# A two-layer attention and mixture-of-experts kernel: six experts with fixed blocks in place of four

## The chip, the cores and the metric

The kernel runs on one core of a Trainium2 chip. The metric is the device time of one execution in microseconds (us). The compute engines are PE (TensorE, with its weight loads shown as PEld), DVE (VectorE), ACT (ScalarE) and POOL (GpSimd). SP (SyncE) issues most of the DMAs, and POOL issues the indirect ones.

## What is computed

Two layers run over 384 tokens of width 1024 (three tiles of 128). Each layer is attention followed by a mixture of experts, and everything around the change lies in the second part:

```
scores = sigmoid(x @ w_router)                    # 384 x 64
pick the top 6 of 64 experts per token (by groups), weights normalised and scaled
for each expert e, over the tokens that picked it:
    gu = x[tok] @ w_gu[e]                         # 1024 x 512
    y  = (silu(gu[:, :256]) * gu[:, 256:]) @ w_down[e]   # 256 x 1024
routed[tok] += weight * y
out = layer_norm(alpha * x + gate * (routed + shared_expert(x)))
```

384 tokens with 6 experts each make 2304 rows over 64 experts, 36 per expert in the mean. An expert's weights are 2 MB (gate and up) and 1 MB (down) in float32, so every layer reads 192 MB of them.

## The kernel before, in words

**Blocks.** Rows are worked on in blocks of 128 rows. `plan_blocks` (line 40) makes the list. The first PRE = 4 blocks hold experts 0 to 3 alone, with 128 rows each. The other 60 experts are ranked by how many rows they got, and the ranks fill 28 blocks of three kinds: one expert with 128 rows, two with 64 each, or three with 64, 32 and 32. The order is (3, 1, 3, 2, 3, 1, 2), four times over. That makes NB = 32 blocks. The experts have a load number n from 0 to 63 in the order of the blocks; `LOADS` gives the rank that belongs to n, and `BLOCK_OF[n]` its block.

**Two ways to the rows of a block.** For the first PRE experts the slots come early: DVE writes a one-hot matrix per expert and tile (L1499), PE multiplies it with a column triple (L1039), DVE turns the outcome into indices (L1512, L1513), and POOL gathers (L1923, from the loop at L1934). All other experts go through memory: DVE works out the order of the experts and a place for each of a token's six choices (up to L1559), POOL scatters 18 sets of entries into `slots` (L1939), waits for them (L1942), loads the table back (L1944), DVE takes it apart (L1569, L1570, in `take_slots` at block 2), and only then can POOL gather block 4 and the later ones (L1951, after `slots_ready`). The gathered rows alternate between two buffers, `xg[0]` and `xg[1]`; blocks 2 and 3 use `gateb` in place of them.

**One block on PE** (loop at L1133): `gate_up(b)` (L1079: 8 steps over the width, each with one, two or four matmuls side by side, which run at once on parts of the array), `turn_rows(b+1)` (L1066, transposes of the next block's gathered rows), `down_rows(b-1)` (L1103), `turn_hidden(b)` (L1089). `gate_up(b)` waits for its weights; `turn_rows` waits for the gather. From block 8 to block 30 every second block also carries a step of the shared expert (L1116, L1121, L1128).

**Weights.** Gate-and-up weights go through a ring of NG = 4 buffers, down weights through ND = 6. SP issues in one fixed order. Before the routing it loads gate-and-up 0 to 3 and down 0 to 3 (L681 to L687). Then it waits for the order of the experts (`order_ready`) and for the entries (L702), loads down 4 and 5, and from there goes block by block: the down weights of block b (each after `down_rows` of the block that used its buffer, L707), then, after `gate_up(b)` (L711), the gate-and-up weights that go into the buffers which block b has just freed (L713). At block 5 it adds the shared expert's weights, at block 25 the vectors of the last normalisation. In layer 0 it goes on with two pieces of the next layer's input projection (L725).

**After the blocks** the results, scattered to memory by POOL (L1929), are read back (L741), summed by PE (L1186) and DVE, and normalised.

Of the kernel before, what the change touches and what calls it, by code (L numbers as in the profile page):

```python
# [16 lines left out]
TILES = 3  # L17
# [12 lines left out]
E = 64  # L30
# [3 lines left out]
FAR = 4096  # L34
NG = 4
ND = 6
PRE = 4


def plan_blocks():  # L40

    blocks = [[(n, P)] for n in range(PRE)]
    wide, half, third = iter(range(PRE, 12)), iter(range(12, 40)), iter(range(40, E))
    for _ in range(4):
        for kind in (3, 1, 3, 2, 3, 1, 2):
            if kind == 1:
                blocks.append([(next(wide), P)])  # L50
            elif kind == 2:
                blocks.append([(next(half), 64), (next(half), 64)])
            else:
                blocks.append([(next(half), 64), (next(third), 32), (next(third), 32)])
    assert all(next(left, None) is None for left in (wide, half, third))
    return blocks
# [5 lines left out]
BLOCK_OF = [n for n, b in enumerate(BLOCKS) for r in b]  # L62
# [130 lines left out]
def build(nc, a, o):  # L193
    soft = [(m, t, h) for t in range(TILES) for m in "BC" for h in (0, 3)]

    with ExitStack() as ctx:
# [58 lines left out]
        xg = [c(DM), c(DM)]  # L255
# [71 lines left out]
        gateb = c(2 * DM).rearrange("p (c d) -> p c d", c=2)  # L327
# [59 lines left out]
        def run_layer(l):  # L387
# [110 lines left out]
            def gather_of(b):  # L498


                if b < PRE:
                    return (xg + [gateb[:, 0, :], gateb[:, 1, :]])[b], first_gathered[b], 16
                return xg[b % 2], gathered[b % 2], 16 * ((b - PRE) // 2 + 1)

            def block_loads(b):
# [28 lines left out]
            def _(sp):  # L534
# [42 lines left out]
                for i in range(EARLY):  # L577
# [16 lines left out]
                    if i == 3:  # L594
                        at, n = CONSTS["empty"]
# [82 lines left out]
                                 ).then_inc(down_ready[n % ND], 16)  # L678

                sp.dma_start(wr, at_layer("w_router").rearrange("a (p k) e -> p (a k) e", p=P)).then_inc(wr_loaded, 16)  # L680
                for n in range(PRE):  # L681
                    if n == 2:
                        for i in range(next_n // 2, next_n):
                            load_mod(NEXT0 + i, MODC + i)
                    emptied(CHUNKS - NG + n)
                    load_gu(n, n)
                    load_down(n, n)  # L687

                sp.wait_ge(order_ready, 1)
                sp.wait_ge(xm_saved, 16 * TILES)  # L690
                sp.wait_ge(xmT_ready, 4 * TILES)
                expert = {}

                def loaded(n):
                    if n not in expert:
                        r = LOADS[n]
                        expert[n] = sp.value_load(by_rank[0:1, r:r + 1], min_val=0, max_val=E - 1)
                    return expert[n]

                for b in range(NB):  # L700
                    if b == 0:
                        sp.wait_ge(entries_ready, 1)  # L702
                        for n in range(PRE, ND):
                            load_down(n, loaded(n))
                    for n in block_loads(b):
                        if n >= ND:
                            sp.wait_ge(y_full, BLOCK_OF[n - ND] + 1)  # L707
                            load_down(n, loaded(n))
                    gu_now = [n for n in range(NG, E) if BLOCK_OF[n - NG] == b]
                    if gu_now:  # L710
                        sp.wait_ge(gu_full, b + 1)  # L711
                    for n in gu_now:
                        load_gu(n, loaded(n))  # L713
                    if b == SHARED_LOAD:
                        sp.wait_ge(residual_ready, TILES)
                        sp.dma_start(shared_gu, at_layer("w_shared_gu").rearrange("a (p k) n -> p (a k) n", p=P)).then_inc(shared_loaded, 16)
                        sp.dma_start(shared_down, at_layer("w_shared_down").rearrange("a (k p) n -> p (a k) n", p=P)).then_inc(shared_loaded, 16)
                    if b == NORM_LOAD:
                        sp.wait_ge(sgu_full, TILES)
                        load_norm(1, G2)  # L720
# [1179 lines left out]
            def _(pool):  # L1900
# [19 lines left out]
                def gather(b):  # L1920

                    rows_in, landed, count = gather_of(b)
                    pool.indirect_dma_start(rows_in, None, scratch_x, bass.IndirectOffsetOnAxis(ap=slot_idx[:, 0, b:b + 1], axis=0),  # L1923
                                            bounds_check=TOK - 1, oob_is_err=False).then_inc(landed, 16)
# [6 lines left out]

                pool.wait_ge(xm_saved, 16 * TILES)
                pool.wait_ge(first_ready, 1)
                for b in range(PRE):  # L1934
                    gather(b)
                pool.wait_ge(table_empty, 16)
                pool.wait_ge(entries_ready, 1)
                for j in range(TILES * TOPK):
                    pool.indirect_dma_start(slots, bass.IndirectOffsetOnAxis(ap=place_i[:, j:j + 1], axis=0),  # L1939
                                            entry[:, j, :], None, bounds_check=P * NCOL - 1, oob_is_err=False  # L1940
                                            ).then_inc(entries_sent, 16)
                pool.wait_ge(entries_sent, 16 * TILES * TOPK)  # L1942
                by_row = slots.rearrange("(p c) v -> p c v", c=NCOL)
                pool.dma_start(table, by_row[:, 0:NB, :]).then_inc(table_loaded, 16)  # L1944
# [77 lines left out]
```

## Time and profile before

| what | value |
|---|---|
| median of 3 runs | 1990.85 us (1979.93 to 1992.41) |
| the profiled execution's own time | 1993.09 us |
| its span, first to last instruction | 1991.4 us |
| mean granted TensorE clock | 0.862 of full speed |
| PE / DVE / ACT / POOL busy | 78% / 28% / 16% / 10% of the span |
| DMA | 576.84 MB, 290 GB/s in the mean |

The profile cuts the span in 40 slices of 49.8 us. In two runs of slices (the tenth to the nineteenth and the thirtieth to the thirty-eighth) DMA is at 90% or more and moves 320 to 425 GB/s: these are the blocks of experts of the two layers. Matmuls are pipelined, so a busy PE is not PE at its peak.

### The profile page before, as it was taken

The page shows a single profiled execution, that of the slowest core. Times are in us where ns is not written, and L with a number is a line of the kernel's source. Part 1 is how long each engine was busy: PE and PEld are TensorE (multiplying, and loading weights), DVE is VectorE, ACT ScalarE, POOL GpSimd, SP SyncE. Part 2 cuts the span into 40 slices and gives each one's busy share as a digit, 9 for nine tenths or more (in the row PEclk, how much of TensorE's full clock was granted, in tenths as well). Part 3 has the DMA queues.
Part 4 walks back from the last instruction along what each step waited for, and adds up shares of the span by engine and source line. Part 5 has one row for each costly group of instructions (what it writes and reads, how often), then busy time and mean ns, then how long its engine had stood idle before and what let it go on. Part 6 is the DMA issues. An engine that isn't in the chain of part 4 may idle for free. (4 is left out here: it accounts for less than half of the span.)

```text
span 1991.4 us, 20055 instructions
## 1 busy us (share of the span) xinstructions
PE 1555.8 (78%) x7633; PEld 796.9 (40%) x7633; DVE 555.6 (28%) x1120; ACT 319.9 (16%) x626; POOL 200.8 (10%) x196
## 2 busy tenths in 40 slices
PE   4797998798587886986669889878758768788684
PEld 1586564453132332332238756545313323233231
DVE  0534332551011111111373444166101101111125
ACT  0322341210000000000122324311000000000000
POOL 0000000051011011100101000004201101101100
PEclk8897699788799898988789979987879988889797
DMA  7624345558999999999845443363599999999965
GB/s 291 190 105 179 131 143 217 226 194 320 417 417 417 395 407 412 408 379 410 325 152 153 143 172 101 126 249 138 210 425 405 414 416 406 398 395 397 418 265 221
DMA packets 114687, 576.84 MB, mean 290 GB/s; under 512 B 41662, under 2 KB 44238, under 8 KB 73500
## 3 DMA queue, kind: packets, MB, share of 16 engines
q1 hardware_dynamic: 94012, 534.36, 67.5%
q0 software_dynamic: 20512, 41.09, 5.5%
q8 instruction: 63, 1.03, 0.2%
q14 instruction: 36, 0.29, 0.0%
q10 hardware_dynamic: 64, 0.07, 0.0%
HBM read 565.10 MB, written 40.39 MB: 304 GB/s over the span
## 5 line engine op out<-in xcount | busy, mean ns | idle before, releaser
L1079 PE MATMUL bank<-ring,arena_a 128*32 128x512 f32 (+2 forms) x2432 | 520.7, 698 | 224.8 <-DMA ring<-in_w_expert_gu 221.7
L1079 PEld LDWEIGHTS bank<-ring,arena_a 128*32 128x32 f32 (+2 forms) x2432 | 174.9, 146 | 537.4 <-issue 537.4
L1608 DVE SCALAR_TENSOR_TENSOR arena_a<-arena_a,slot_w,bank 128x256 f32<-128x256 f32 x64 | 30.8, 481 | 649.2 <-ACT arena_a L1859 646.3
L1103 PE MATMUL bank<-arena_b,arena_a 128*32 128x512 f32 (+2 forms) x800 | 205.8, 599 | 3.0 <-DVE arena_a L1617 3.0
L1859 ACT ACTIVATE arena_a<-bank 128x256 f32<-128x256 f32 x64 | 24.7, 386 | 907.6 <-PE bank L1079 907.6
L1929 POOL DMA_INDIRECT scratch_y<-arena_a,slot_idx x64 | 65.9, 1030 | 920.2 <-DVE arena_a L1625 919.0
L858 PE MATMUL bank<-win_hi,xmT_hi 128*128 128x512 f32 (+1 forms) x288 | 109.0, 379 | 16.3 <-DVE arena_a L1228 11.2
L1103 PE MATMUL bank<-arena_a 128*32 128x512 f32 (+2 forms) x416 | 116.0, 595 | 0.0
L1624 DVE COPY arena_a<-bank 128x512 f32<-128x512 f32 x64 | 44.3, 692 | 248.8 <-PE bank L1103 248.8
L859 PE MATMUL bank<-win_hi,xmT_lo 128*128 128x512 f32 (+1 forms) x288 | 109.6, 381 | 0.0
L860 PE MATMUL bank<-w_lo,xmT_hi 128*128 128x512 f32 (+1 forms) x288 | 109.1, 379 | 0.0
L998 PE MATMUL bank<-ring,xmT 128*128 128x512 f32 x192 | 86.1, 611 | 6.4 <-ACTq L1818 6.4
L1103 PEld LDWEIGHTS bank<-arena_b,arena_a 128*32 128x32 f32 (+2 forms) x800 | 61.7, 130 | 67.8 <-issue 64.3
L1066 PE MATMUL bank<-cst,arena_a 128*128 128x128 f32 x480 | 68.0, 287 | 17.9 <-DMA arena_a<-scratch_x,slot_idx 17.9
L1066 PEld LDWEIGHTS bank<-cst,arena_a 128*128 128x128 f32 x480 | 55.7, 146 | 60.8 <-issue 43.3
L801 PE MATMUL bank<-ring,condT 128*2 128x512 f32 x384 | 63.7, 782 | 14.3 <-DMA ring<-in_w_mod 14.3
L1923 POOL DMA_INDIRECT arena_a<-scratch_x,slot_idx x60 | 64.0, 1067 | 74.5 <-DVE slot_w L1513 54.3
L1219 DVE TENSOR_TENSOR w_lo<-ring,win_hi 128x2048 fp32r<-128x2048 f32 (+1 forms) x22 | 48.5, 2203 | 79.5 <-ACT win_hi L1724 79.5
L858 PEld LDWEIGHTS bank<-win_hi,xmT_hi 128*128 128x128 f32 x288 | 54.6, 189 | 29.5 <-issue 12.5
L859 PEld LDWEIGHTS bank<-win_hi,xmT_lo 128*128 128x128 f32 x288 | 54.8, 190 | 10.7
L998 PEld LDWEIGHTS bank<-ring,xmT 128*128 128x128 f32 x192 | 37.5, 197 | 53.8 <-issue 46.9
L860 PEld LDWEIGHTS bank<-w_lo,xmT_hi 128*128 128x128 f32 x288 | 54.5, 189 | 10.3
(277 smaller groups left out, 1679.5 us busy)
## 6 DMA issues: line engine op xcount, KB each, us to landing
ring<-in_w_expert_gu SPq DMA_DIRECT2D x128, 2048.0 KB, 14.9
arena_b<-in_w_expert_down SPq DMA_DIRECT2D x88, 1024.0 KB, 22.1
ring<-in_w_mod SPq DMA_DIRECT2D x24, 2048.0 KB, 7.9
arena_a<-in_w_expert_down SPq DMA_DIRECT2D x40, 1024.0 KB, 20.5
ring<-in_w_in SPq DMA_DIRECT2D x10, 2048.0 KB, 14.2
ring<-in_w_out SPq DMA_DIRECT2D x4, 2048.0 KB, 7.7
ring<-scratch_y SPq DMA_DIRECT2D x4, 2048.0 KB, 10.9
arena_b<-scratch_y SPq DMA_DIRECT2D x8, 1024.0 KB, 17.1
```

Of the source, the lines that this page charges most:

```text
L801: ins = pe.matmul(bank[32 * j:32 * j + 2, :], condT[:, k, :], w[:, k % 2, CH * j:CH * j + CH], start=(k == 0 and not first), stop=(k + 1 = ...
L858: pe.matmul(out, hi[:, k, :], win_hi[:, k, cols], start=(k == 0), stop=False)
L859: pe.matmul(out, lo[:, k, :], win_hi[:, k, cols], start=False, stop=False)
L860: ins = pe.matmul(out, hi[:, k, :], w_lo[s][:, k, cols], start=False, stop=(k == KD - 1))
L998: ins = pe.matmul(bank[:, :], xmT[:, k, P * t:P * t + P], w[:, k, :], start=(k == 0), stop=(k == KD - 1))
L1066: ins = pe.transpose(psum[2 + k // 4][:, P * (k % 4):P * (k % 4) + P], rows_in[:, P * k:P * k + P], ident)
L1079: ins = pe.matmul(psum[b % 2][r:r + w, :], xT[:, k, r:r + w], ring_view(gu_slot(n))[:, k, :], start=(k == 0), stop=(k == KD - 1))
L1103: ins = pe.matmul(psum[5 + f][r:r + w, :], hT[b % 2][:, k, r:r + w], down[n % ND][:, k, CH * f:CH * f + CH], start=(k == 0), stop=(k == 1))
L1219: dve.tensor_tensor(w_lo[s][:, ks, cols], ring_view(s)[:, ks, cols], win_hi[:, ks, cols].bitcast(F32), ALU.subtract).then_inc(win_lo_ready, 1)
L1624: dve.tensor_copy(ys[b % 2][:, 0:CH], psum[5][:, :])
L1923: pool.indirect_dma_start(rows_in, None, scratch_x, bass.IndirectOffsetOnAxis(ap=slot_idx[:, 0, b:b + 1], axis=0), bounds_check=TOK - 1, o ...
L1929: pool.indirect_dma_start(scratch_y, bass.IndirectOffsetOnAxis(ap=slot_idx[:, 1, b:b + 1], axis=0), ys[b % 2], None, bounds_check=TOK * TO ...
```

## The change

PRE goes from 4 to 6: experts 4 and 5 get blocks of their own with 128 rows and have their slots from one-hots too. The constant HELD = 4 keeps what PRE = 4 meant for the loads and gathers that come first. The other 58 experts are spread over nine blocks of one, eight of two and eleven of three, so NB goes from 32 to 34. In SP's order the gate-and-up weights of expert 4 are issued right after `gate_up(0)`, ahead of the wait for the entries and of down 4 and 5. POOL gathers blocks 4 and 5 after the 18 scatters of entries and before it waits for them; each of the two gathers waits for transposes of earlier blocks.

```diff
-PRE = 4
+PRE = 6
+HELD = 4
...
     blocks = [[(n, P)] for n in range(PRE)]
-    wide, half, third = iter(range(PRE, 12)), iter(range(12, 40)), iter(range(40, E))
-    for _ in range(4):
-        for kind in (3, 1, 3, 2, 3, 1, 2):
+    wide, half, third = iter(range(PRE, 15)), iter(range(15, 42)), iter(range(42, E))
+    for kinds in ((3, 1, 3, 2, 3, 1, 2), (3, 1, 3, 2, 1, 3, 2), (3, 1, 2, 3, 1, 3, 2), (3, 1, 2, 3, 1, 2, 1)):
+        for kind in kinds:
...
-                    return (xg + [gateb[:, 0, :], gateb[:, 1, :]])[b], first_gathered[b], 16
+                    return (xg + [gateb[:, 0, :], gateb[:, 1, :]] + xg)[b], first_gathered[b], 16
...
-                for n in range(PRE):
+                for n in range(HELD):
...
-                sp.wait_ge(order_ready, 1)
-                sp.wait_ge(xm_saved, 16 * TILES)
-                sp.wait_ge(xmT_ready, 4 * TILES)
                 expert = {}
 
                 def loaded(n):
+                    if n < PRE:
+                        return n
+                    if not expert:
+                        sp.wait_ge(order_ready, 1)
...
                     if b == 0:
+                        sp.wait_ge(gu_full, 1)
+                        load_gu(HELD, HELD)
+                        sp.wait_ge(xm_saved, 16 * TILES)
+                        sp.wait_ge(xmT_ready, 4 * TILES)
                         sp.wait_ge(entries_ready, 1)
-                        for n in range(PRE, ND):
+                        for n in range(HELD, ND):
                             load_down(n, loaded(n))
...
-                    gu_now = [n for n in range(NG, E) if BLOCK_OF[n - NG] == b]
+                    gu_now = [n for n in range(HELD + 1, E) if BLOCK_OF[n - NG] == b]
...
-                for b in range(PRE):
+                for b in range(HELD):
                     gather(b)
...
+                for b in range(HELD, PRE):
+                    pool.wait_ge(xT_full, b - 1)
+                    gather(b)
                 pool.wait_ge(entries_sent, 16 * TILES * TOPK)
```

## Rows read from the trace of the kernel before

**Rows 1.** Page, section 5: gate-and-up matmuls, all forms together

```profile
L1079 PE MATMUL bank<-ring,arena_a 128*32 128x512 f32 (+2 forms) x2432 | 520.7, 698 | 224.8 <-DMA ring<-in_w_expert_gu 221.7
```

**Rows 2.** Windows: us, busy by engine, clock, DMA share, GB/s, from routing to stream end

```profile
402.00:476.00 74.00, 66.04 (x248) 33.07 (x249) 29.17 (x55) 9.97 (x20) 30.89 (x30) 0.88 0.58 208
476.00:968.00 492.00, 381.89 (x1983) 143.60 (x1981) 68.86 (x124) 39.97 (x83) 53.15 (x52) 0.88 0.99 408
1361.00:1440.00 79.00, 64.38 (x233) 31.70 (x234) 29.18 (x55) 9.72 (x18) 31.18 (x30) 0.87 0.56 199
1440.00:1922.00 482.00, 370.39 (x1951) 140.73 (x1951) 66.71 (x121) 39.42 (x81) 52.92 (x52) 0.87 0.99 408
```

**Rows 3.** Timeline of PE, layer 0, blocks 2 to 4: start, us, line

```profile
431.30 7.03 PE L1079 MATMUL bank<-ring,arena_a 128*128 128x512 f32 x16
442.69 7.03 PE L1079 MATMUL bank<-ring,arena_a 128*128 128x512 f32 x16
454.68 1.97 PE L1066 MATMUL bank<-cst,arena_a 128*128 128x128 f32 x8 [4.96 <-DMA arena_a<-scratch_x,slot_idx]
469.06 1.09 PE L1066 MATMUL bank<-cst,arena_a 128*128 128x128 f32 x8
```

**Rows 4.** Timeline of PE, layer 1, blocks 3 and 4

```profile
1401.71 7.03 PE L1079 MATMUL bank<-ring,arena_a 128*128 128x512 f32 x16
1419.65 1.97 PE L1066 MATMUL bank<-cst,arena_a 128*128 128x128 f32 x8 [10.91 <-DMA arena_a<-scratch_x,slot_idx]
1432.83 1.09 PE L1066 MATMUL bank<-cst,arena_a 128*128 128x128 f32 x8
```

**Rows 5.** Timelines of DVE and PE, layer 1: the one-hots and what waits for them

```profile
1353.74 3.17 DVE L1499 TENSOR_SCALAR arena_a<-cst,cmisc,arena_a 128x128 f32<-128x128 f32 x12
1354.75 5.25 PE L1039 MATMUL bank<-cmisc,arena_a 128*128 128x3 f32 x24 [1.25 <-DVE arena_a L1499]
1360.04 0.17 DVE L1512 TENSOR_SCALAR slot_idx<-bank 128x8 int32<-128x8 f32 x1 [2.11 <-PE bank L1039]
```

**Rows 6.** Timelines of POOL and DVE, entries, table and gathers of both layers

```profile
439.05 0.98 POOL L1939 DMA_INDIRECT slots<-arena_a,place_i  x1 [0.30 <-issue]
445.98 0.60 POOL L1944 DMA_DIRECT2D arena_a<-slots  x1 [5.95 <-DMA slots<-arena_a,place_i]
448.14 0.20 DVE L1569 CAST slot_idx<-arena_a 128x56 int32<-128x56 f32 x1 [1.45 <-DMA arena_a<-slots]
449.23 1.04 POOL L1923 DMA_INDIRECT arena_a<-scratch_x,slot_idx  x1 [1.35 <-DVE slot_w L1570]
1398.07 0.98 POOL L1939 DMA_INDIRECT slots<-arena_a,place_i  x1 [0.30 <-issue]
1409.29 1.05 POOL L1923 DMA_INDIRECT arena_a<-scratch_x,slot_idx  x1 [1.77 <-issue]
```

**Rows 7.** Timeline of SP, layer 0: issues of weights around the first blocks

```profile
416.02 1.48 SPq L677 DMA_DIRECT2D arena_a<-in_w_expert_down  x2
417.90 32.91 SPq L673 DMA_DIRECT2D ring<-in_w_expert_gu  x4
469.91 2.53 SPq L673 DMA_DIRECT2D ring<-in_w_expert_gu  x3
```

**Rows 8.** Windows as in rows 2, two stretches in which the stream falls back

```profile
850.00:870.00 20.00, 19.89 (x102) 7.16 (x103) 2.10 (x4) 1.47 (x3) 2.02 (x2) 0.85 0.81 322
1820.00:1830.00 10.00, 10.00 (x66) 3.89 (x59) 2.10 (x4) 1.48 (x3) 0.00 (x0) 1.00 0.78 294
```

**Rows 9.** Timeline of PE, layer 1, gate-and-up of the last three blocks

```profile
1893.13 8.77 PE L1079 MATMUL bank<-ring,arena_a 128*32 128x512 f32 x64 [4.68 <-DMA ring<-in_w_expert_gu]
1906.71 7.03 PE L1079 MATMUL bank<-ring,arena_a 128*128 128x512 f32 x16
1920.20 7.09 PE L1079 MATMUL bank<-ring,arena_a 128*64 128x512 f32 x32
```

**Rows 10.** Page, section 3: queue of the indirect DMAs, packets, MB, share

```profile
q0 software_dynamic: 20512, 41.09, 5.5%
```

## The prediction

> **What bounds the kernel now.** I read the slices first: in both layers the stretch of the expert blocks has DMA near full. The windows turn that into numbers: from 476 to 968 us and from 1440 to 1922 us the DMA share is 0.99 at 408 GB/s [rows 2]. The groups confirm it from PE's side: its gate-and-up matmuls stood idle for 221.7 us until a load of expert weights landed [rows 1]. So each layer's middle is a stream of bytes, and the change moves the same 192 MB. At 408 GB/s one expert (3.146 MB) takes 7.7 us and one piece of 1.049 MB takes 2.6 us.
>
> What can change is the two ends of the stream. At its head DMA is only 0.58 and 0.56 busy over 74 and 79 us [rows 2]: four gate-and-up buffers are full, and one comes free per block. There PE sets the pace, with 11.39 us from one single-expert block to the next (431.30 to 442.69) [rows 3]. Then block 4 stands until its gather has landed: idle 4.96 us in layer 0 [rows 3], 10.91 us in layer 1 [rows 4]. From the end of block 3's gate-and-up to that of block 4's it took 469.06 - 449.72 = 19.3 us and 1432.83 - 1408.74 = 24.1 us; without a wait it is 11.4, so the table's way costs 7.9 and 12.7 us, 20.6 in all. The waits are 15.9 of this; the other 4.7 us are matmuls on a slower clock behind them (eight transposes took 1.97 us where others take 1.09). The last block's end, then a fixed read-back and normalisation, close each layer.
>
> **The change part by part.** The sum goes against the profiled execution's own 1993.09 us.
>
> *Six more one-hots and their products, on the path.* DVE spends 3.17 us on 12 one-hots, 0.26 each, but PE needs 5.25 us for the products of 12, 0.44 each, and DVE then waits 2.11 us for them [rows 5]. So PE is later, and 6 more cost 6 x 0.44 = 2.6 us per layer (the other end is DVE's 1.6). Nothing covers it: DVE's chain to the entries and the first gathers both hang on this result, so every time below shifts by 2.6.
>
> *Gathers 4 and 5 inside POOL's queue.* They stand behind the 18 scatters and ahead of the wait for them. The last scatter starts at 439.05 and takes 0.98 plus 0.30 [rows 6], so gather 4 is issued at 442.9 after the shift. Its wait, for block 2's transposes (three turned), and that of gather 5 for block 3's are met by then: block 3's rows are turned right after block 2's gate-and-up, at about 431.30 + 7.03 + 1.1 + 2.6 = 442.0. What is queued behind is the wait for the entries, the table load, the first scatters of results and gather 6. The two issues take some 2.7 us, and the wait for the entries was 5.95 us long [rows 6], so they are hidden but for the shift; DVE got its table at 448.14 [rows 6] and would have it by about 451, against 452.3 when block 3's gate-and-up ends. No stall there: 0.
>
> How long gather 4 takes I bound by the two seen: issued 449.23, transposed from 454.68, 5.5 us; issued 1409.29, transposed from 1419.65, 10.4 us, the latter beside scatters and weights [rows 3, 4, 6]. PE wants it at 452.3. With 5.5 it lands 3.9 us early, with 10.4 one us late. I take early, since few weights move just then, and keep the other end as a rival. The Trainium skill, page "DMA: Bandwidth & Descriptors", section "Anatomy of one DMA", gives about 2 us fixed plus bytes at 436 GB/s for such a DMA, an estimate of 3.2 us for 512 KB: by it the gather is never late. Both rows are longer, so the rows decide.
>
> *Where the stream starts.* Before, it runs full from the end of block 4, the first triple: at 469.91 SP issues three buffers at once [rows 7]. By then gate-and-up 0 to 7 and down 0 to 6 are in. After, blocks 4 and 5 are single and free one buffer each; the stream is full from the end of block 5's gate-and-up, when gate-and-up 9, the shared weights and down 6 to 8 (8.4 MB, 20 us) queue up, more than PE needs to free three more buffers. Block 5's end is block 3's end plus two periods and the shift: 449.72 + 22.8 + 2.6 = 475.1 in layer 0, 6.0 later than 469.06; 1408.74 + 22.8 + 2.6 = 1434.1 in layer 1, 1.3 later than 1432.83. By then gate-and-up 0 to 8 and down 0 to 5 are in: one gate-and-up more, one down less, 1.049 MB ahead, 2.6 us. So +3.4 and -1.3, together +2.1 us. The removed wait is thus eaten by two blocks that use 3 MB each in 11.4 us where the stream could bring 4.6. The early issue of gate-and-up 4, ahead of down 4 and 5 [rows 7], is worth nothing: block 4 needs it 30 us later.
>
> *The middle.* Same bytes. The stream falls back where a triple follows a pair, by up to 0.19 x 20 = 3.8 or 0.22 x 10 = 2.2 us [rows 8]; such neighbours go from seven per layer to six. Bounds: nothing, or a share of 0.01 of 974 us [rows 2], -10 us. I take -1 per layer, -2.
>
> *The tail.* The last triple's start hangs on its weights (idle 4.68 us), and from there PE runs on its own: 1893.13, 1906.71, 1920.20 [rows 9]. Behind the last triple there are now three blocks (1, 2, 1) in place of two (1, 2). The bytes up to the triple are one expert fewer, so it starts 7.7 us sooner; PE then does one block more, 11.4 us. From the triple's start to the last gate-and-up's end that was 34.2 us and becomes 45.6; the remaining stream of 15.7 MB takes 38.5, so PE sets the end. 11.4 - 7.7 = +3.7 per layer, +7.4. Bounds: 0, if the stream sets the tail, and 11.4 per layer, if the earlier start is lost.
> The Trainium skill, same page, section "Bandwidth", says that for HBM to SBUF the HBM side, about 358 GB/s, binds. The trace shows 408, so I don't use it; by 358 an expert would take 8.8 us, and the sum below would be some 5.6 in place of 8.5.
>
> *More packets.* Two blocks per layer make two gathers and two scatters of 128 slots more, 1024 packets in both layers, without more rows. The software queue's 20512 packets took 5.5% of 16 engines' span, 85 ns each [rows 10], so at most 1024 x 85 / 16 = 5.4 us; most of that time is full rows, and empty slots may cost nothing. I take +1. The reserve path for overfull experts is not run before; the new list has at least the room of the old at every rank, so it stays unrun.
>
> Sum: 2.1 - 2 + 7.4 + 1 = +8.5, so 2001.6 us. The median shown lies 2.2 us under the profiled execution; on its scale this is **1999 us**, slower by 0.4%. A measurement of this kernel tells about 1% from no change, so this counts as no change.
>
> **The rivals.**
> *The removed waits come off whole* (faster). If what runs behind block 4 is set by when PE hands buffers back, and not by bytes, the 20.6 us go: -20.6 + 5.2 (shift) + 7.4 - 2 + 1 = -9, 1982 us. For it: the fall-backs in the stream, where PE held the buffers [rows 8]. Against: 221.7 us of PE waiting for weights [rows 1]. Chance 0.15.
> *PE becomes the bound* (slower). Two blocks more per layer are 4 x 11.4 = 45.6 us of PE; if the stream keeps up, they count whole: 45.6 - 20.6 + 5.2 = +30, 2021 us. It decides once the mean block's weights take less time than PE's block: now 58 experts in 28 blocks are 2.07 x 7.7 = 16 us against 11.4, or 13 where the clock is slow (8.77 in place of 7.03 for the gate-and-up [rows 9]). PE has 221.7 us to spare [rows 1]. Chance 0.12.
> *Gather 4 is late all the same*: the change then does not do what it says. With the longer landing PE waits 1 us per layer, and the slower clock behind a wait costs 2 to 3 more [rows 3, 4]: +8, 2007 us. Chance 0.15.
>
> **How the numbers follow.** The forecast as it stands has 0.53, its own range 1993 to 2007; 0.05 is left for what I don't see. The range is to hold the rival with the late gather and the one with the waits gone, and reaches toward the bound on PE: 1982 to 2015. Slower by over 1% (above 2010.8) is the PE rival and a tail of lost starts: 0.14. Faster by over 1% (under 1970.9) needs the removed waits and the -10 of the middle at once: 0.05. The rest is 0.81.
>
> **What would show it.** In the profile after: one-hots and their products 2.6 us longer, and the first gather that much later; no wait of PE for the gather at block 4; two more single blocks at 11.4 us; the end of block 5's gate-and-up at about 475 us in layer 0; from there a DMA share of 0.99 at about 408 GB/s; from the last triple's start to the last gate-and-up's end some 46 us. I am wrong if PE's idle time for weights shrinks by much more than 45 us, if the stream's rate moves, or if PE still waits for a gather.

## The result, and the profile after

The changed kernel took 2002.1 us (median of 11 runs, 1992.5 to 2008.46), the kernel before, run beside it, 1986.17 us (11 runs). The ratio is 1.0077, with a 95% interval of 1.0051 to 1.0103: slower by 0.8%, clear of the noise, but under the 1% below which the prediction counts a difference as no change. The forecast was slower by 0.4%. The profiled execution took 2005.57 us, with a span of 2003.9 us. Line numbers in the changed kernel are 6 higher from `turn_rows` on, and 9 higher from the load of the table on.

To compare kernels I use one measure for each layer, the **stretch**: from the start of the first one-hot (DVE) to the end of the last gate-and-up (PE). Before, in layer 1, that is 1920.20 + 7.09 - 1353.74 = 573.6 us [rows 5, 9]. The part from layer 0's end of stretch to layer 1's first one-hot I call the **gap** (the end of layer 0, and layer 1's attention). The diff doesn't touch the gap.

PE's timeline in both layers of the changed kernel, blocks 3 to 5 and the first matmuls after them (answers to [rows 3, 4]):

```profile
441.77 7.03 PE L1085 MATMUL bank<-ring,arena_a 128*128 128x512 f32 x16
448.64 1.04 PE L1072 MATMUL bank<-cst,arena_a 128*128 128x128 f32 x8
453.17 7.03 PE L1085 MATMUL bank<-ring,arena_a 128*128 128x512 f32 x16
460.04 1.04 PE L1072 MATMUL bank<-cst,arena_a 128*128 128x128 f32 x8
464.56 7.03 PE L1085 MATMUL bank<-ring,arena_a 128*128 128x512 f32 x16
471.43 1.04 PE L1072 MATMUL bank<-cst,arena_a 128*128 128x128 f32 x8
...
1432.44 1.04 PE L1072 MATMUL bank<-cst,arena_a 128*128 128x128 f32 x8
1436.97 7.03 PE L1085 MATMUL bank<-ring,arena_a 128*128 128x512 f32 x16
1443.84 1.04 PE L1072 MATMUL bank<-cst,arena_a 128*128 128x128 f32 x8
```

No line carries an idle time: both gather waits are gone. The singles follow one another every 11.4 us. Block 5's gate-and-up ends at 464.56 + 7.03 = 471.6, which is 80.8 us after the layer's first one-hot (390.83); in layer 1 it is 1444.0 - 1362.93 = 81.1 us.

All engines' timeline, layer 1, the one-hots and what waits for them (answers to [rows 5]):

```profile
1362.93 4.71 DVE L1505 TENSOR_SCALAR arena_a<-cst,cmisc,arena_a 128x128 f32<-128x128 f32 x18
1363.93 7.81 PE L1045 MATMUL bank<-cmisc,arena_a 128*128 128x3 f32 x36 [1.26 <-DVE arena_a L1505]
1371.78 0.17 DVE L1518 TENSOR_SCALAR slot_idx<-bank 128x12 int32<-128x12 f32 x1 [3.13 <-PE bank L1045]
```

From the first one-hot to the indices it takes 8.85 us, where it took 6.30 [rows 5].

The timelines of POOL and DVE, layer 0 (answers to [rows 6]):

```profile
439.42 1.04 POOL L1929 DMA_INDIRECT arena_a<-scratch_x,slot_idx  x1 [0.30 <-issue]
440.77 1.01 POOL L1929 DMA_INDIRECT arena_a<-scratch_x,slot_idx  x1 [0.31 <-issue]
445.19 0.59 POOL L1953 DMA_DIRECT2D arena_a<-slots  x1 [3.41 <-DMA slots<-arena_a,place_i]
447.95 0.46 DVE L1575 CAST slot_idx<-arena_a 128x56 int32<-128x56 f32 x1 [2.18 <-DMA arena_a<-slots]
```

Gathers 4 and 5 fill time that POOL had spent on waiting: the wait for the entries shrinks from 5.95 to 3.41 us. DVE has the table 447.95 - 390.83 = 57.1 us after the first one-hot; before it was 448.14 - 394.73 = 53.4 us.

The windows of the head of each layer and of the stream from there to the start of the last triple (columns as in [rows 2]):

```profile
398.00:472.00 74.00, 70.95 (x228) 37.57 (x229) 29.68 (x57) 10.33 (x21) 33.01 (x31) 0.91 0.56 197
472.00:920.00 448.00, 336.22 (x1785) 130.18 (x1783) 62.98 (x115) 37.52 (x78) 51.48 (x50) 0.88 0.98 407
1363.00:1444.00 81.00, 76.29 (x236) 42.45 (x237) 34.99 (x80) 9.71 (x18) 32.65 (x31) 0.87 0.51 184
1444.00:1892.00 448.00, 338.71 (x1788) 131.20 (x1786) 62.96 (x115) 37.90 (x78) 51.49 (x50) 0.88 0.98 405
```

The stream before, up to the same point:

```profile
476.00:928.00 452.00, 342.74 (x1789) 129.26 (x1787) 58.52 (x109) 36.48 (x75) 50.61 (x50) 0.87 0.99 409
1440.00:1893.00 453.00, 341.51 (x1789) 129.47 (x1787) 58.50 (x109) 36.48 (x75) 50.38 (x50) 0.87 0.99 408
```

The middle is a stream of bytes at nearly the same rate as before: 407 and 405 GB/s where it was 409 and 408.

The page, its queue of indirect DMAs and its gate-and-up group (answers to [rows 1, 10]):

```profile
q0 software_dynamic: 21664, 41.10, 5.5%
...
L1085 PE MATMUL bank<-ring,arena_a 128*32 128x512 f32 (+2 forms) x2400 | 523.8, 658 | 219.2 <-DMA ring<-in_w_expert_gu 216.1
```

1152 packets more, where 1024 were worked out, and the same 5.5%. PE's idle time for gate-and-up weights fell by 5.6 us only: four more blocks of PE work were not paid out of it.

PE's timeline, layer 1, the last four gate-and-ups (answers to [rows 9]):

```profile
1892.87 8.98 PE L1085 MATMUL bank<-ring,arena_a 128*32 128x512 f32 x64 [9.39 <-DMA ring<-in_w_expert_gu]
1908.38 7.03 PE L1085 MATMUL bank<-ring,arena_a 128*128 128x512 f32 x16
1920.15 7.09 PE L1085 MATMUL bank<-ring,arena_a 128*64 128x512 f32 x32
1931.76 7.03 PE L1085 MATMUL bank<-ring,arena_a 128*128 128x512 f32 x16
```

From the last triple's start to the end, 1931.76 + 7.03 - 1892.87 = 45.9 us; before, 34.2.

**Where the time went.** The stretches take 575.5 and 575.9 us where they took 569.4 and 573.6: +8.4 us in sum. The span grew by 12.5. The other 4.1 lie outside the diff: -3.9 ahead of the first one-hot, +1.0 after layer 1's stretch, and +7.0 in the gap, 396.6 in place of 389.6 us. The -3.9 can't be put down to the change: a second profile of the changed kernel (e8 below) has its first one-hot at 385.33 in place of 390.83 us. Counted from the first one-hot on, the two profiles are 16.4 us apart, and the medians 15.9.

### The profile page after: what moved, and what is told of

The parts are those of the page before. It is cut to its first block and busy times, and to the rows that moved or that the text cites. A ratio compares the mean times of both kernels' runs of the same rounds, so it can differ in the third digit from the quotient of the medians.

```text
span 2003.9 us, 20147 instructions
## 1 busy us (share of the span) xinstructions
PE 1581.9 (79%) x7649; PEld 822.5 (41%) x7649; DVE 564.9 (28%) x1148; ACT 325.5 (16%) x638; POOL 209.9 (10%) x204
## 5 line engine op out<-in xcount | busy, mean ns | idle before, releaser
L1085 PEld LDWEIGHTS bank<-ring,arena_a 128*32 128x32 f32 (+2 forms) x2400 | 182.7, 143 | 523.7 <-issue 523.7
L1109 PE MATMUL bank<-arena_b,arena_a 128*32 128x512 f32 (+2 forms) x848 | 213.3, 611 | 9.3 <-DMA arena_b<-in_w_expert_down 6.6
L1935 POOL DMA_INDIRECT scratch_y<-arena_a,slot_idx x68 | 70.4, 1035 | 924.3 <-DVE arena_a L1631 901.4
L864 PE MATMUL bank<-win_hi,xmT_hi 128*128 128x512 f32 (+1 forms) x288 | 110.2, 383 | 16.6 <-DVE arena_a L1234 11.4
L1109 PEld LDWEIGHTS bank<-arena_b,arena_a 128*32 128x32 f32 (+2 forms) x848 | 68.3, 136 | 104.6 <-issue 101.4
L1109 PE MATMUL bank<-arena_a 128*32 128x512 f32 (+2 forms) x352 | 79.9, 595 | 0.0
L1929 POOL DMA_INDIRECT arena_a<-scratch_x,slot_idx x64 | 69.3, 1082 | 79.0 <-DVE slot_w L1519 60.1
L807 PE MATMUL bank<-ring,condT 128*2 128x512 f32 x384 | 61.5, 757 | 14.6 <-DMA ring<-in_w_mod 14.6
L864 PEld LDWEIGHTS bank<-win_hi,xmT_hi 128*128 128x128 f32 x288 | 54.9, 191 | 29.4 <-issue 12.5
L1192 PE MATMUL bank<-ring,cst 128*128 128x512 f32 x64 | 33.0, 681 | 34.2 <-DMA arena_b<-scratch_y 34.2
L865 PEld LDWEIGHTS bank<-win_hi,xmT_lo 128*128 128x128 f32 x288 | 55.2, 192 | 10.6
## 6 DMA issues: line engine op xcount, KB each, us to landing
ring<-in_w_in SPq DMA_DIRECT2D x10, 2048.0 KB, 14.2
```

What stands on the lines that cost most here:

```text
L807: ins = pe.matmul(bank[32 * j:32 * j + 2, :], condT[:, k, :], w[:, k % 2, CH * j:CH * j + CH], start=(k == 0 and not first), stop=(k + 1 = ...
L864: pe.matmul(out, hi[:, k, :], win_hi[:, k, cols], start=(k == 0), stop=False)
L865: pe.matmul(out, lo[:, k, :], win_hi[:, k, cols], start=False, stop=False)
L1085: ins = pe.matmul(psum[b % 2][r:r + w, :], xT[:, k, r:r + w], ring_view(gu_slot(n))[:, k, :], start=(k == 0), stop=(k == KD - 1))
L1109: ins = pe.matmul(psum[5 + f][r:r + w, :], hT[b % 2][:, k, r:r + w], down[n % ND][:, k, CH * f:CH * f + CH], start=(k == 0), stop=(k == 1))
L1192: ins = pe.matmul(psum[2 * t + f][:, :], ident, back_rows[t][k][:, CH * f:CH * f + CH], start=(k == 0), stop=(k == SUMMED - 1))
```

## The experiments

My theory: the stretch is a head that PE paces, a middle that the stream paces, and a tail that PE paces; what the change takes off the head it gives back in one-hots, single blocks and tail. Rivals: PE is the bound everywhere, so that each added block costs 11.4 us; the gathers or the table still decide the head. All kernels start from the changed one. All in one table, every time from the timelines of PE and DVE of one profile each; head, and the last triple's start, are counted from the layer's first one-hot (head: end of the last block before the first triple, except before, where it is the end of the first triple, block 4; tail: from the last triple's start to the end of the stretch).

| kernel | stretch, layers 0 / 1 | head | last triple's start | tail | gap | ratio to before (95%) |
|---|---|---|---|---|---|---|
| before | 569.4 / 573.6 | 74.4 / 79.2 | 534.1 / 539.4 | 35.3 / 34.2 | 389.6 | 1 |
| after | 575.5 / 575.9 | 80.8 / 81.1 | 530.0 / 529.9 | 45.6 / 45.9 | 396.6 | 1.0077 (1.0051 to 1.0103) |
| e1 last blocks 1, 2 | 572.7 / 572.0 | 80.7 / 80.7 | 536.2 / 535.2 | 36.5 / 36.7 | 386.4 | 1.0023 (1.0000 to 1.0046) |
| e2 32 blocks | 573.0 / 571.0 | 80.8 / 80.8 | 537.9 / 537.0 | 35.1 / 34.0 | 389.4 | 1.0009 (0.9989 to 1.0029) |
| e3 36 blocks | 590.1 / 590.1 | 93.6 / 92.4 | 544.9 / 545.5 | 45.2 / 44.5 | 386.8 | 1.0175 (1.0140 to 1.0209) |
| e4 four fixed | 579.1 / 578.8 | 83.5 / 83.2 | 533.7 / 532.5 | 45.4 / 46.3 | 396.4 | 1.0171 (1.0130 to 1.0212) |
| e5 table of 228 columns | 589.6 / 585.3 | 93.6 / 89.7 | 543.9 / 538.6 | 45.7 / 46.7 | 396.7 | 1.0173 (1.0119 to 1.0228) |
| e6 36 blocks, 230 columns | 577.2 / 578.1 | 80.9 / 79.9 | 532.9 / 533.2 | 44.3 / 44.9 | 390.7 | 1.0055 (1.0025 to 1.0085) |
| e7 five fixed | 567.3 / 567.4 | 68.7 / 68.8 | 533.3 / 533.2 | 34.0 / 34.2 | 388.2 | 0.9950 (0.9922 to 0.9977) |
| e8 after, again | 575.5 / 575.9 | 80.7 / 81.1 | 529.9 / 529.9 | 45.5 / 45.9 | 396.5 | 1.0085 (1.0055 to 1.0115) |
| e9 gathers behind the table | 577.6 / 575.2 | 81.5 / 80.7 | 530.8 / 529.4 | 46.8 / 45.8 | 388.3 | 1.0038 (1.0008 to 1.0068) |
| e10 loads in the old order | 575.4 / 576.0 | 80.7 / 81.1 | 529.9 / 530.2 | 45.5 / 45.8 | 396.6 | 1.0046 (1.0019 to 1.0072) |
| e11 cycles exchanged | 577.7 / 575.6 | 80.7 / 80.7 | 530.9 / 530.1 | 46.8 / 45.5 | 388.2 | 1.0046 (1.0022 to 1.0071) |
| e12 five, last block 2 | 571.8 / 569.6 | 68.8 / 68.8 | 541.1 / 540.2 | 30.7 / 29.4 | 390.5 | 0.9969 (0.9946 to 0.9991) |

**e1: the tail alone.**

```diff
-    ..., (3, 1, 2, 3, 1, 3, 2), (3, 1, 2, 3, 1, 2, 1)):
+    ..., (3, 1, 2, 3, 1, 3, 2), (3, 1, 2, 1, 3, 1, 2)):
```

> The changed kernel with its last cycle as (3, 1, 2, 1, 3, 1, 2), so that two blocks and not three follow the last triple, as in the kernel before. My theory (the stream of weights sets the middle, PE the tail): the last triple starts 7.7 us later in each layer and one block of 11.4 us less follows, so the stretch from the first one-hot to the end of the last gate-and-up is 3.7 us shorter per layer than in the changed kernel (575.5 and 575.9 us there, so 571.8 and 572.2), and the whole about 7.4 us faster than the changed kernel. Rival (PE is the bound): the same blocks in another order, no difference. Rival (the stream hides the tail): no difference either.

The stretches came out within 0.9 us of the 571.8 and 572.2 expected. PE's timeline, layer 1:

```profile
1879.05 8.77 PE L1085 MATMUL bank<-ring,arena_a 128*32 128x512 f32 x64 [2.10 <-DMA ring<-in_w_expert_gu]
1892.33 7.03 PE L1085 MATMUL bank<-ring,arena_a 128*128 128x512 f32 x16
1907.00 8.79 PE L1085 MATMUL bank<-ring,arena_a 128*64 128x512 f32 x32 [2.82 <-DMA ring<-in_w_expert_gu]
```

The last triple starts 6.2 and 5.3 us later, short of one expert's 7.7, and one block less stands behind it. That takes 9.1 and 9.2 us off the tail and not 11.4, since the pair at the end now waits for its weights (2.82 us in layer 1). Both differences nearly cancel: -2.8 and -3.9 per layer, where the tail's term said 3.7.

**e2: two blocks fewer.** The other 58 experts in six blocks of one, eight of two and twelve of three; the last blocks are 1, 2 as in e1.

```diff
-    wide, half, third = iter(range(PRE, 15)), iter(range(15, 42)), iter(range(42, E))
-    for kinds in ((3, 1, 3, 2, 3, 1, 2), (3, 1, 3, 2, 1, 3, 2), (3, 1, 2, 3, 1, 3, 2), (3, 1, 2, 3, 1, 2, 1)):
+    wide, half, third = iter(range(PRE, 12)), iter(range(12, 40)), iter(range(40, E))
+    for kinds in ((3, 1, 3, 2, 3, 2), (3, 1, 3, 2, 3, 2), (3, 1, 3, 2), (3, 1, 3, 2), (3, 1, 2, 3, 1, 2)):
```

> Six fixed experts, but the other 58 in 26 blocks (6 of one, 8 of two, 12 of three), so 32 blocks in all, ending in a triple, a single and a pair. My theory: within 3 us per layer of the run with the tail (1, 2), since the middle is bound by bytes: stretches of 569 to 575 us. Rival (PE is the bound): two blocks fewer per layer take 22.8 us off each stretch, 45 us off the whole.

Against e1, which ends alike, two blocks fewer change the stretches by +0.3 and -1.0 us. If PE were the bound they would take 22.8 off.

**e3: two blocks more.** Twelve of one, eight of two, ten of three.

```diff
-    for kinds in ((3, 1, 3, 2, 3, 1, 2), (3, 1, 3, 2, 1, 3, 2), (3, 1, 2, 3, 1, 3, 2), (3, 1, 2, 3, 1, 2, 1)):
+    for kinds in ((3, 1, 3, 2, 1, 3, 1, 2), (3, 1, 3, 2, 1, 1, 3, 2), (3, 1, 2, 3, 1, 1, 2), (3, 1, 2, 3, 1, 2, 1)):
```

(and 18, 44 in place of 15, 42 for the bounds of the three kinds.)

> Six fixed experts and 30 blocks for the others (12 of one, 8 of two, 10 of three), 36 in all, with the added singles in the middle and the changed kernel's tail. My theory: 0 to 4 us per layer longer than the changed kernel (575.5 and 575.9 us), the small loss where two singles follow each other. Rival (PE is the bound): 22.8 us per layer longer, 45 us in all.

A miss: +14.6 and +14.2 us per layer. But the table shows where: the head is 12.8 and 11.3 us longer, though up to block 5 this kernel has the same blocks and the same loads as the changed one. POOL's wait for the entries took 13.46 us in place of 3.41, and gather 4 was late. One thing differs there: the number of columns of the slot table, which is the number of blocks plus 192, so 228 in place of 226.

**e5: the columns alone, and e6: the 36 blocks with other columns.**

```diff
-NCOL = NB + PASSES * E
+NCOL = NB + PASSES * E + 2
...
-                    pool.dma_start(over_table, by_row[:, NB:NCOL, :]).then_inc(over_loaded, 16)
+                    pool.dma_start(over_table, by_row[:, NB:NB + PASSES * E, :]).then_inc(over_loaded, 16)
```

> The changed kernel with two columns more, never used, in each row of the slot table: 228 in place of 226, so a row of it in DRAM is 2736 bytes (as with 36 blocks) in place of 2712. Blocks, loads and order of work stay. Theory pitch (the entries' small writes land late because of where they lie): their median time from issue to landing rises from 5.8 to about 9 us, the transposes of block 4 wait about 10 us for its gather, block 5's gate-and-up ends about 92 us after the first one-hot in place of 80.8, the stretch from the first one-hot to the last gate-and-up is about 587 us per layer in place of 575.7, the time about 23 us over the changed kernel's. Rival (the late gather came from the 36 blocks themselves): landing 5.8 us, block 5's end 80.8, stretch 575.7, time of the changed kernel within 5 us.

> The 36 blocks again, with two unused columns in each row of the slot table: 230 in place of 228 (2760 bytes a row in place of 2736). Theory pitch: the entries land in a median of about 6 us, block 4's gather is in time, block 5's gate-and-up ends about 81 us after the first one-hot, and what is left of the two blocks more is the middle: stretches of 576 to 580 us per layer, time 22 to 28 us under that of the first 36-block kernel. Rival (36 blocks make the start late by themselves): stretches of 590 again and the same time. A stretch of 599 with an early start would be TensorE as the bound (two blocks of 11.4 us in full).

Two columns that nothing uses made the changed kernel's stretches 14.1 and 9.4 us longer; two more made those of the 36 blocks 12.9 and 12.0 us shorter. In e5, POOL's and PE's timelines, layer 0:

```profile
436.64 1.04 POOL L1929 DMA_INDIRECT arena_a<-scratch_x,slot_idx  x1 [0.30 <-issue]
...
452.50 0.59 POOL L1953 DMA_DIRECT2D arena_a<-slots  x1 [13.49 <-DMA slots<-arena_a,place_i]
...
457.41 1.97 PE L1072 MATMUL bank<-cst,arena_a 128*128 128x128 f32 x8 [10.11 <-DMA arena_a<-scratch_x,slot_idx]
```

The gather was issued as early as ever; PE stood 10.11 us for it and could turn its rows at 457.41, over 20 us after the issue. The DMA view, 400 to 445 us, gives the median time from issue to landing (the last number) of three loads of gate-and-up weights and of the 18 scatters of entries; in e5, and then in e6:

```profile
ring<-in_w_expert_gu SPq DMA_DIRECT2D x3, 2048.0 KB, 16.0
...
slots<-arena_a,place_i POOLq DMA_INDIRECT x18, 9.9
```

```profile
ring<-in_w_expert_gu SPq DMA_DIRECT2D x3, 2048.0 KB, 8.3
...
slots<-arena_a,place_i POOLq DMA_INDIRECT x18, 5.6
```

The windows of 22 us in which the entries are written (columns as in [rows 2]), again e5 and then e6:

```profile
416.00:438.00 22.00, 22.00 (x82) 11.44 (x81) 7.96 (x11) 4.27 (x10) 16.81 (x18) 1.00 1.02 262
```

```profile
415.00:437.00 22.00, 22.00 (x71) 11.07 (x71) 7.77 (x10) 3.53 (x9) 17.12 (x17) 1.00 0.74 291
```

With 228 columns the writes landed late, and the DMA engines were busy all the time (share 1.02) and moved less (262 GB/s in place of 291). So this is the rival "gather 4 is late all the same", which the changed kernel escapes with its 226 columns; the step from 32 blocks (224) to 34 could have met it. And e6 settles the other rival: with the head in time, two blocks more cost 1.7 and 2.2 us per layer over the changed kernel, and not 22.8.

**e4: the early slots alone taken back.** Four fixed experts with the blocks of the change; the gate-and-up weights that block 4 multiplies with are those of expert 4, whichever ranks first. Its output is thus not the layer's; the bytes and the work are the same.

```diff
-PRE = 6
+PRE = 4
...
-    blocks = [[(n, P)] for n in range(PRE)]
+    blocks = [[(n, P)] for n in range(6)]
```

(and `range(6, 15)` for the first kind.)

> The 34 blocks of the changed kernel in their order, with PRE = 4: blocks 4 and 5 are single experts by rank, whose rows come by way of the table. My theory: the one-hots take 2.5 us less per layer, and PE's wait for the gather at block 4 is back with the slow clock behind it, 7.9 us in layer 0 and 12.7 in layer 1: stretches of about 581 and 586 us, the whole some 15 us slower than the changed kernel. Rival (the waits were hidden behind the stream anyway): 5 us faster than the changed kernel, by the one-hots alone.

The waits come back, at 4.03 and 3.19 us; PE's timeline, both layers:

```profile
450.39 1.97 PE L1072 MATMUL bank<-cst,arena_a 128*128 128x128 f32 x8 [4.03 <-DMA arena_a<-scratch_x,slot_idx]
...
1425.42 1.18 PE L1072 MATMUL bank<-cst,arena_a 128*128 128x128 f32 x8 [3.19 <-DMA arena_a<-scratch_x,slot_idx]
```

The head grows by 2.7 and 2.1 us, with 2.6 us of one-hots saved in it, so the wait and the slower matmuls behind it are worth some 5 us. The direction is as expected, the size for layer 1 is not: the 10.91 us of [rows 4] did not come again. The timed ratio is further up than the 6.5 us of the two stretches; four runs stand behind it, and I have no reading for the rest.

**e9: the place in POOL's queue.**

```diff
-                for b in range(HELD, PRE):
-                    pool.wait_ge(xT_full, b - 1)
-                    gather(b)
                 pool.wait_ge(entries_sent, 16 * TILES * TOPK)
...
                 pool.dma_start(table, by_row[:, 0:NB, :]).then_inc(table_loaded, 16)
+                for b in range(HELD, PRE):
+                    pool.wait_ge(xT_full, b - 1)
+                    gather(b)
```

> The changed kernel with the gathers of blocks 4 and 5 issued behind the load of the table in place of ahead of the wait for the entries; slots by one-hots, blocks and loads stay. Theory (the place in POOL's queue is what takes the wait away, the early slots alone are not): gather 4 is issued some 6.6 us later, about 446 us in layer 0, lands 5.5 to 10.4 us after that, PE's transposes of block 4 wait 3 to 8 us for it and run on at the lower clock, the stretch is 579 to 586 us per layer in place of 575.7, the time 6 to 20 us over the changed kernel's. Rival (the gather has slack enough): no wait, 575.7, the same time.

My theory fell here, the rival holds. Timelines of POOL and PE, layer 0:

```profile
445.61 1.05 POOL L1929 DMA_INDIRECT arena_a<-scratch_x,slot_idx  x1 [0.31 <-issue]
...
448.90 1.09 PE L1072 MATMUL bank<-cst,arena_a 128*128 128x128 f32 x8 [0.58 <-DMA arena_a<-scratch_x,slot_idx]
```

Issued 6.6 us later (55.2 us after the first one-hot in place of 48.6), the gather landed within 3.3 us, and the head lost 0.7 us in layer 0 and nothing in layer 1. Having the slots early is what counts; the place among the scatters is worth little.

**e10: the order of SP's loads.**

```diff
-                        sp.wait_ge(gu_full, 1)
-                        load_gu(HELD, HELD)
                         sp.wait_ge(xm_saved, 16 * TILES)
...
                             load_down(n, loaded(n))
+                        sp.wait_ge(gu_full, 1)
+                        load_gu(HELD, HELD)
```

> The changed kernel with expert 4's gate-and-up weights loaded behind the down weights of experts 4 and 5 again, as before. Theory (block 4 needs them 30 us later, so the order is worth nothing): stretches of 575.7 us per layer within 1 us, no new wait at block 4. Rival (the early load keeps the stream fuller at its head): stretches longer by up to 2.6 us per layer, the time of a megabyte of weights at 408 GB/s.

575.4 and 576.0: worth nothing, as priced.

**e8 and e11: the gap.** e8 is the changed kernel unaltered. e11:

```diff
-    for kinds in ((3, 1, 3, 2, 3, 1, 2), (3, 1, 3, 2, 1, 3, 2), (3, 1, 2, 3, 1, 3, 2), (3, 1, 2, 3, 1, 2, 1)):
+    for kinds in ((3, 1, 3, 2, 3, 1, 2), (3, 1, 2, 3, 1, 3, 2), (3, 1, 3, 2, 1, 3, 2), (3, 1, 2, 3, 1, 2, 1)):
```

> The changed kernel unaltered, once more. In its first profile the part between the two stretches (layer 0's last blocks and output, layer 1's attention), whose code did not change, took 396.5 us against 386 to 390 in the kernel before and in three of the four other runs, because TensorE stayed at its lower clock, 0.50, for 18 us more near 1190 us. Theory chance: 386 to 390 us this time, stretches 575.7 each, span about 1995 us. Rival (the shift of the work in time brings it): 396 us again, span about 2003 us.

> The changed kernel with its second and third cycle of blocks exchanged: same blocks, same bytes, same head and tail. Asked is the clock of layer 1's attention. Theory phase (which stretch runs at the lower clock hangs on the exact time at which layer 0 ends, and the changed kernel happens to end it badly): the stretches move by 2 us at most, and the part between them takes 386 to 391 us where the changed kernel took 396.5 twice; the time then falls by about 7 us. Rival (it hangs on the head, the tail or the slot table, which this kernel shares): 396.5 us again, time of the changed kernel.

e8 repeats the stretches and the gap to 0.1 us, so the long gap is not the chance of one execution. In e11 the stretches move by +2.2 and -0.2, and the gap is 388.2. Windows of layer 1's attention, first the changed kernel, then e11, at the same distance from the end of layer 0's stretch (212 to 242 us after it; columns as in [rows 2], so the third number from the right is the granted clock):

```profile
1178.00:1184.00 6.00, 2.44 (x24) 1.97 (x22) 3.28 (x15) 3.31 (x13) 0.00 (x0) 0.95 0.50 128
1184.00:1196.00 12.00, 11.85 (x52) 8.15 (x51) 6.15 (x18) 5.76 (x26) 0.00 (x0) 0.50 0.70 298
1196.00:1208.00 12.00, 11.92 (x49) 7.79 (x47) 4.30 (x11) 2.72 (x10) 0.00 (x0) 0.50 0.40 142
```

```profile
1178.60:1184.60 6.00, 2.44 (x13) 2.03 (x13) 2.79 (x15) 3.76 (x19) 0.00 (x0) 0.77 0.68 200
1184.60:1196.60 12.00, 11.75 (x62) 7.75 (x61) 7.07 (x20) 4.74 (x21) 0.00 (x0) 0.69 0.62 261
1196.60:1208.60 12.00, 11.40 (x62) 7.09 (x61) 5.04 (x16) 3.73 (x13) 0.00 (x0) 0.74 0.51 176
```

In both PE had just been idle (2.44 us busy of 6). In the changed kernel it then runs 24 us at 0.50, the level of 1.2 GHz, though it is busy 99% of that time; in e11 it comes back to full speed in between, and does 124 matmuls where the other does 101. Of the 14 profiles five show the long half-speed stretch and a gap of 396.4 to 396.7 (after, e4, e5, e8, e10), the other nine 386.4 to 390.7. How the schedule decides it the runs don't show: layer 0's stretch was 575.4 to 589.6 us where the gap was long, and 567.3 to 590.1 where it was not. Layer 0's tail, in the table, was 45.4 to 45.7 us in these five and in no other, but that was noticed afterwards and is no proof of a cause. The timed executions don't confirm the profiles here. e10 has the long gap and e11 the short, and their profiled executions took 2004.46 and 1997.4 us; but their medians, 2000.21 and 1999.11 us, are only 1.1 us apart. Whether the timed executions all have the gap of their profile stays open.

**e7: five fixed experts.** Between four, which wait for the table, and six.

```diff
-PRE = 6
+PRE = 5
...
-    wide, half, third = iter(range(PRE, 15)), iter(range(15, 42)), iter(range(42, E))
-    for kinds in ((3, 1, 3, 2, 3, 1, 2), (3, 1, 3, 2, 1, 3, 2), (3, 1, 2, 3, 1, 3, 2), (3, 1, 2, 3, 1, 2, 1)):
+    wide, half, third = iter(range(PRE, 13)), iter(range(13, 42)), iter(range(42, E))
+    for kinds in ((3, 1, 3, 2, 3, 1, 2), (3, 1, 3, 2, 3, 1, 2), (3, 1, 3, 2, 3, 1, 2), (3, 2, 1, 2, 3, 1, 2)):
...
-NCOL = NB + PASSES * E
+NCOL = NB + PASSES * E + 1
...
-                    pool.wait_ge(scattered[i], 16 * (NB // 2))
+                    pool.wait_ge(scattered[i], 16 * ((NB + 1 - i) // 2))
...
```

> Five fixed experts, 33 blocks, rows of the slot table kept at 226 columns; last blocks a single and a pair. Against the kernel with six and the same last blocks (stretches 572.7 and 572.0 us): the one-hots take 1.3 us less, and block 5, the first that is filled by the table, begins at the earliest some 57 us after the first one-hot, by when its gather has landed if the table comes as early as in the changed kernel. Theory (the stream bounds the middle, and the fixed experts only have to bridge the table): no wait for a gather at block 5, stretches of 567 to 571 us, time 1981 to 1988 us, the best of all or equal to the kernel before. Rival (the table is late for block 5 as it was for block 4 in the kernel before): a wait of 2 to 8 us at block 5, stretches of 573 to 579 us, time 1991 to 2000 us.

POOL's and PE's timelines, layer 0:

```profile
440.38 1.04 POOL L1929 DMA_INDIRECT arena_a<-scratch_x,slot_idx  x1 [2.52 <-DVE slot_w L1576]
...
452.54 1.04 PE L1072 MATMUL bank<-cst,arena_a 128*128 128x128 f32 x8
457.16 7.07 PE L1085 MATMUL bank<-ring,arena_a 128*32 128x512 f32 x64
```

Gather 5, the first by the table, is issued 12 us before its transposes and nobody waits for it. The stretches are 567.3 and 567.4, the time 1978.32 us (10 runs): faster than the kernel before, ratio 0.9950 (0.9922 to 0.9977), and the lowest ratio in the table.

**e12: five fixed, one block behind the last triple.** The last cycle is (3, 2, 1, 2, 1, 3, 2).

> Five fixed experts, with the last cycle (3, 2, 1, 2, 1, 3, 2) in place of (3, 2, 1, 2, 3, 1, 2), so that one block stands behind the last triple and not two. By the working of the tail the last triple starts one expert's bytes later, 7.7 us, and TensorE has one block of 11.4 us less behind it: -3.7 us per layer, stretches of 563 to 565 us where the other order gave 567.4, time some 7 us less, about 1971 us. Rival (the pair behind the triple waits for a buffer that the triple still holds, 5 us for its load): the gain is lost, stretches of 567 to 569 us and the same time as the first kernel with five fixed experts.

The rival holds. PE's timeline, layer 1:

```profile
1888.79 7.07 PE L1085 MATMUL bank<-ring,arena_a 128*32 128x512 f32 x64
1909.65 8.50 PE L1085 MATMUL bank<-ring,arena_a 128*64 128x512 f32 x32 [9.10 <-DMA ring<-in_w_expert_gu]
```

The last triple starts 7.8 and 7.1 us later than in e7, near one expert's 7.7, but the pair behind it waits 9.10 us for its weights, more than the 5 us that the rival named. The stretches are 571.8 and 569.6 us, longer than e7's by 4.5 and 2.2. A single between the triple and the pair, as in e7, covers the pair's load.

## Why the prediction was right, and where it was short

- *What bounds the kernel.* Right. With the head in time, 32, 34 and 36 blocks differ by some 2 us per layer (e2 to e1, e6 to after), so PE is not the bound, and its rival of 2021 us falls.
- *One-hots, +2.6 per layer.* Right: 8.85 - 6.30 = 2.55 us, set by PE's products, which ran at the granted clock 0.50 in both kernels.
- *Gathers inside POOL's queue, 0.* Right: no wait. From the first one-hot the table came 3.7 us later, the shift of 2.6 and 1.1 more, still in time. e9 shows that the place matters less than I thought.
- *Start of the stream.* Right: block 5's end was to be 6.0 later than block 4's before in layer 0 and 1.3 in layer 1; on the scale of the first one-hot it is 6.4 and 1.9. This refutes the rival in which the removed waits come off whole: two single blocks at 11.4 us ate them. By the same working a fixed expert more costs 11.4 - 7.7 = 3.7 us per layer at the head and 1.3 for its one-hots. From six to five that is 5.0. e1 to e7, which end alike, measured 5.4 and 4.6, but in part by luck: 2.5 us of each lie in the tail, where e1's pair waits and e7's does not, and the last triple starts only 2.9 and 2.0 sooner. Against e2, whose pair doesn't wait either, e7's last triple starts 4.6 and 3.8 sooner.
- *Middle, -1 per layer.* The last triple's start moved by -4.2 and -9.5 us. The terms gave -7.7 + 3.4 - 1 = -5.3 and -7.7 - 1.3 - 1 = -10.0. Right to about 1 us.
- *Tail, +3.7.* Right: 45.6 and 45.9 us against the 45.6 forecast, and e1 takes it back, with smaller parts on both sides. The 34.2 us that the working started from are layer 1's; layer 0's tail before was 35.3, so it grew by 10.2 and 11.8.
- *Packets, +1.* The queue's share did not move; two blocks fewer (e2) gained nothing that shows. Nearer to 0.
- *The order of SP's loads, 0.* Right (e10).
- *Gather 4 late all the same.* Not in the changed kernel, but in e5: +23.5 us in the two stretches, where I had priced +8. The price was for a slow landing of one gather; e5 slowed the weights and the 18 scatters with it.

The stretches together came out at +8.4 us, where +8.5 were forecast. That they agree to 0.1 us is partly luck: up to the last triple's start the terms were 1.7 us too low in sum, the tail's 0.8 and the packets' 1 too high.

The whole was short: +8.5 forecast, +15.9 measured. That 1999 us lies only 3.1 under the measured median is luck too, since the 1990.85 us of three runs on which it stands are 4.7 us above the 1986.17 of eleven. The step that was short is one that I didn't write down: that all outside the stretches stays as it was. In the profiles the gap took 7.0 us more, with PE at the lower clock; 8.4 + 7.0 = 15.4 us would be nearly the whole of the 15.9. Two profiles of the changed kernel show this. What sets off the lower clock, and, by e10 and e11, how far every timed execution has the long gap, stays open.

## What to carry to other kernels

Where a fixed head bridges the time until a table arrives, each step of it costs what it takes beyond the stream's own pace, so take as many as bridge the table and no more: here four waited, six overpaid, five beat both. Order the end so that what runs on behind the last wait for the stream is short, but keep a block that covers the load of the next. And compare kernels stage by stage: here an unchanged stage ran slower at a lower clock, and two unused columns in a table made PE wait 10 us for a gather.

## What the runs showed of the hardware that I had not expected

- With rows of 228 columns of 12 bytes (2736 bytes) in the slot table, small scattered writes were slow: median 9.9 us to landing (e5) against 5.6 with 2760 bytes (e6), with DMA 1.02 busy at 262 GB/s. In the kernels with rows of 2688 (before, e2), 2712 and 2760 bytes the median was 5.4 to 6.6 us. The Trainium skill, page "DMA: Bandwidth & Descriptors", section "Latency and other measured facts", knows row pitches in HBM at large powers of two as slow for large copies; 2736 is no such pitch, and no run here tried one. Whether it is the pitch as such or the place in memory of what lies behind the table was not tried.
- PE at 1.2 GHz for 24 us while 99% busy (granted clock 0.50), in the same place in two profiles of the same kernel (after and e8) and in e4, e5 and e10, and gone in the profile in which two cycles of the layer before were exchanged (e11).
